# An encoder layer in one kernel: the first half rebuilt around contraction chunks and pairs of token tiles

## The reference, cut to what matters

```python
mod = (jax.nn.silu(c) @ w_ada + b_ada).reshape(bsz, 1, N_MOD, d)          # w_ada: 1024 x 6144
sh1, sc1, g1, sh2, sc2, g2 = (mod[:, :, i] for i in range(N_MOD))
h = x * (1 + sc1) + sh1
z = h @ w_in                                                              # 1024 x 1536: u | v | p
za = jax.nn.gelu(z[..., :2 * A_WIDTH])
u, v = za[..., :A_WIDTH], layer_norm(za[..., A_WIDTH:], v_norm_g, v_norm_b)
v = einsum('hqp,bnphc->bnqhc', w_spatial, v) + b_spatial.T[:, :, None]    # chunks of 128 tokens, 4 heads
a_out = u * v
pooled = multiscale_pool(z[..., 2 * A_WIDTH:])      # centred mean over 2, 4, 8, 16 tokens minus the token
b_out = einsum('bsgc,gcd->bsgd', pooled, w_pool) * pool_scale
mix = concatenate([a_out, b_out], axis=-1) @ w_out
x = layer_norm(ALPHA * x + g1 * mix, ln1_g, ln1_b)
h = x * (1 + sc2) + sh2
# then: routing to 2 of 32 experts for each token, the experts, and a last layer norm
```

## Time and profile before

| | |
|---|---|
| three runs | 1457.67, 1460.60, 1460.58 us (median 1460.58) |
| profiled execution, its own time | 1457.56 us |
| profiled execution, span from first to last instruction | 1455.8 us |
| TensorE busy, mean granted clock | 1266.5 us (87%), 0.940 |
| weight loads (PEld), VectorE, ScalarE, GpSimd busy | 1030.7, 932.9, 653.3, 280.3 us |
| HBM read, written | 297.47 MB, 39.37 MB |

### The profile page before, as it was taken

How to read it: one execution, slowest core, us unless ns; L and a number is a source line. 1 busy time by engine, 2 the same in 40 slices (tenths; PEclk the granted TensorE clock), 3 DMA queues, 4 the chain that set the end, 5 groups by cost and what they waited for, 6 DMA issues and landing times.

```text
span 1455.8 us, 22916 instructions
## 1 busy us (share of the span) xinstructions
PE 1266.5 (87%) x6239; PEld 1030.7 (71%) x6240; DVE 932.9 (64%) x1025; ACT 653.3 (45%) x635; POOL 280.3 (19%) x321
## 2 busy tenths in 40 slices
PE   4479999999789799426999999999999999999592
PEld 3367888788668588325888888888888888888440
DVE  7655544443356455595657875765478888888188
ACT  5532322111212112215556765665478888887222
POOL 6100000000024344241111211111112111222122
PEclk9889999999989899558999999999999999999896
DMA  9642231000233432634769996877689999998793
GB/s 296 246 143 93 96 102 57 18 29 1 92 125 116 144 115 101 243 132 168 263 245 344 402 366 226 307 261 269 226 342 396 398 397 395 388 406 310 307 348 138
DMA packets 111712, 329.44 MB, mean 226 GB/s; under 512 B 12192, under 2 KB 37952, under 8 KB 111680
## 3 DMA queue, kind: packets, MB, share of 16 engines
q1 hardware_dynamic: 98288, 288.63, 53.4%
q0 software_dynamic: 11520, 34.09, 6.3%
q10 hardware_dynamic: 1872, 6.29, 1.1%
HBM read 297.47 MB, written 39.37 MB: 231 GB/s over the span
## 4 chain that ended last, share of the span: by engine, by line
PE 77%; DVE 14%; DMA 3%; issue 2%; ACT 2%; POOL 1%; SPq 1%; DVEq 0%; POOLq 0%; ACTq 0%
PE bank L1320 21%; PE bank L1322 21%; PE bank L1321 21%; PE bank L1552 2%; PE bank L1342 1%; PE bank L1343 1%; PE bank L1516 1%; PE bank L1574 1%; DVE ada_l L944 1%; DVE hT L968 1%; DVE fin L1284 1%; DVE fin L1299 1%; DVE gated L1280 1%; PE bank L1407 1%; ACT ada_h L693 1%
## 5 line engine op out<-in xcount | busy, mean ns | idle before, releaser
L1220 DVE TENSOR_TENSOR gu_l<-gu_raw,gu_h x124 | 278.5, 2287 | 39.7 <-ACT gu_h L815 39.7
L1320 PE MATMUL bank<-gu_h,xT_h 128*128 (+1 forms) x624 | 248.1, 398 | 4.1 <-DVE xT_l L1239 4.1
L1322 PE MATMUL bank<-gu_h,xT_l 128*128 (+1 forms) x624 | 244.5, 392 | 0.0
L1321 PE MATMUL bank<-gu_l,xT_h 128*128 (+1 forms) x624 | 243.9, 391 | 0.0
L815 ACT ACTIVATE gu_h<-gu_raw (+1 forms) x128 | 238.4, 1924 | 5.2 <-issue 5.2
L1224 DVE TENSOR_TENSOR dn_l<-dn_raw,dn_h (+1 forms) x64 | 143.6, 2285 | 5.9 <-ACT dn_h L819 5.9
L1320 PEld LDWEIGHTS bank<-gu_h,xT_h 128*128 128x128 f32 x624 | 117.8, 189 | 28.1 <-DVE xT_l L1239 2.9
L1320 PE MATMUL bank<-win_h,hT_h 128*128 128x512 f32 x288 | 117.4, 408 | 22.5 <-DMA pool_s<-in_pool_scale 22.5
L1322 PEld LDWEIGHTS bank<-gu_h,xT_l 128*128 128x128 f32 x624 | 117.7, 189 | 25.5
L1321 PEld LDWEIGHTS bank<-gu_l,xT_h 128*128 128x128 f32 x624 | 118.0, 189 | 23.7
L819 ACT ACTIVATE dn_h<-dn_raw (+1 forms) x64 | 119.0, 1914 | 33.9 <-DVE table_i L1215 33.8
(11 more groups left out here) (226 smaller groups left out, 2144.5 us busy)
## 6 DMA issues: line engine op xcount, KB each, us to landing
gu_raw<-in_w_gate_up SPq DMA_DIRECT2D x128, 1024.0 KB, 7.5
dn_raw<-in_w_down SPq DMA_DIRECT2D x64, 1024.0 KB, 7.5
ada_raw<-in_w_ada SPq DMA_DIRECT2D x24, 1024.0 KB, 5.5
y<-y_rows SPq DMA_DIRECT2D x24, 512.0 KB, 5.4
win_raw<-in_w_in SPq DMA_DIRECT2D x8, 768.0 KB, 6.9
h_rows<-h SPq DMA_DIRECT2D x12, 512.0 KB, 2.7
x_rows<-x SPq DMA_DIRECT2D x12, 512.0 KB, 3.6
fin<-x_rows SPq DMA_DIRECT2D x12, 512.0 KB, 13.7
```

Source lines behind the costliest of these rows:

```text
L1220: nv.tensor_tensor(gu_slot(gu_l, e, c), gu_slot(gu_raw, e, c), gu_slot(gu_h, e, c).bitcast(F32), ALU.subtract).then_inc(S["gu_split_l"], 1)
L1320: mm(out, lh, rh, start=start, stop=False)
L1321: mm(out, lh, rl, start=False, stop=False)
L1322: return mm(out, ll, rh, start=False, stop=stop)
```

## The change

The first half, up to the mix stage, is rebuilt. Everything behind the mix of the last tile stays.

- **Opening by contraction chunk.** x tiles 0 and 1 are loaded and transposed first. For each chunk k of 8, SP loads two blocks of 128 columns of `w_ada` (shift and scale of these 128 channels, 0.5 MB each, rows of 512 bytes) and chunk k of W_in. `ada0_mm(k)` makes the chunk's shift and scale, VectorE and ScalarE modulate and split chunk k of x, and TensorE adds chunk k's products into all of u, v and p of the first pair. TensorE issues `ada0_mm(k + 1)` ahead of chunk k's products. VectorE makes `win_l` of chunk k - 1 in its turn k, behind the modulation of chunk k.
- **float32 conditioning.** `w_ada` is no longer split. Its blocks are the weights (128 x 128, float32) and the two columns of silu(c) are the moving operand: 16 float32 matmuls for 256 columns of `w_ada`, which give columns directly. `mod_columns`, `c_hl`, `pair_sum` and the high and low parts go. Eight blocks are in the opening and 16 late, at fixed points of pairs 1 to 3 (`ADA_POINTS`): seven bursts of two blocks and two of one.
- **Pairs.** The tokens go in 6 pairs of 256. u and p are made transposed, with W_in as weights and 256 moving columns (`chunk`), v as before (`v_part`). The spatial product comes out transposed too, its bias and `v_norm_b` go into an offset made once (`spatial_weights`), so that `a_transposes` and their copy go.
- **Pooling by running sums.** p lies transposed in `pbuf`, VectorE makes the window sums by four additions of shifted columns (`pool_p`), and the band matrices with their products (`pool_mm`) go. The last 8 tokens of a pair wait for the next one; at the end of a request they are made apart (`edge_mm`).
- **W_out in W_in's columns.** Its raw chunks go where u's and p's columns of W_in were, all at once, as soon as the last u and p are made, while v of the last pair is computed. The splits are ahead of the last `norm_v` and `gate_u` on VectorE. `mix(0)` is followed by the last pair's spatial and pool products, then `mix(1)`, then the last `edge_mm`; GpSimd's first `second` waits for that (`fb_made`).

```diff
+ADA_POINTS = {(1, "mid_u"): (0,), (1, "mid_v"): (1, 2), (1, "end_v"): (3, 4),
+              (2, "mid_u"): (5, 6), (2, "mid_v"): (7, 8), (2, "end_v"): (9, 10),
+              (3, "mid_u"): (11, 12), (3, "mid_v"): (13, 14), (3, "end_v"): (15,)}
...
@@ SyncE @@
+            sp.dma_start(xs[:], x_rows(0, 0)).then_inc(S["x_loaded"], 16)
+            sp.dma_start(xs_b[:], x_rows(0, 1)).then_inc(S["x_loaded"], 16)
...
             for k in range(KD):
+                if k >= ADA0_SLOTS:
+                    sp.wait_ge(S["ada_made"], k - ADA0_SLOTS + 1)
+                for m in range(2):
+                    c = m * D + k * P
+                    sp.dma_start(ada0[k % ADA0_SLOTS][:, m], w_ada[:, :, c:c + P]).then_inc(ada0_loaded[k % ADA0_SLOTS], 16)
                 if k >= WIN_SLOTS:
                     sp.wait_ge(S["win_l_made"], k - WIN_SLOTS + 1)
...
+            sp.wait_ge(S["u_made"], 2 * NP)
+            sp.wait_ge(S["p_made"], 2 * NP)
             for k in range(KD):
-                if k >= 4:
-                    sp.wait_ge(S["wout_l_made"], k - 3)
-                elif k == 0:
-                    sp.wait_ge(S["p_made"], NT)
-                sp.dma_start(wout_raw[k % 4][:], w_out[:, k, :]).then_inc(wout_loaded[k], 16)
+                sp.dma_start(wout_raw[:, k, 0::2, :], w_out[:, k, :].rearrange("p (a n) -> p a n", a=2)).then_inc(wout_loaded[k], 16)
@@ GpSimd @@
             plus_one(5)
+            pool.wait_ge(S["fb_made"], 2)
             second(0)
@@ VectorE @@
+            for k in range(KD):
+                dve.wait_ge(S["ada_made"], k + 1)
+                nv.tensor_tensor(mod[:, :, k:2 * KD:KD], ps[6 + k % 2][:, 4 * k:4 * k + 4].rearrange("p (c s) -> p s c", s=2),
+                                 cols[:, None, k:2 * KD:KD].to_broadcast([P, 2, 2]), ALU.add).then_inc(S["mod_made"], 1)
+                dve.wait_ge(S["mod_made"], k + 1)
+                high_gain(k)
+                nv.tensor_scalar(h_raw[0][:, k, :], h_raw[0][:, k, :], gain1[:, 0, k:k + 1], mod[:, 0, k:k + 1], ALU.mult, ALU.add).then_inc(S["k_mod"], 1)
+                if k >= 1:
+                    dve.wait_ge(S["win_h_made"], k)
+                    nv.tensor_tensor(win_l[:, k - 1, :], win_raw[(k - 1) % WIN_SLOTS][:], win_h[:, k - 1, :].bitcast(F32), ALU.subtract).then_inc(S["win_l_made"], 1)
+                dve.wait_ge(S["k_high"], k + 1)
+                nv.tensor_tensor(hT_l[0][:, k, :], h_raw[0][:, k, :], hT_h[0][:, k, :].bitcast(F32), ALU.subtract).then_inc(S["k_low"], 1)
...
+                n = PW - 1
+                for level in range(len(WINDOWS)):
+                    a, b = (pbuf, abuf)[level > 0], 1 << level
+                    st.done(nv.tensor_tensor(abuf[:, level:4, 0:n], a[:, level:4, 0:n], a[:, level:4, b:n + b], ALU.add))
...
+            norm_tile(0, 0, 0, prev=False)
+            edge_out(NP - 1, 6, 2)
@@ TensorE @@
+            def chunk(bank, j, part, k, s, start, stop):
+                out, c = ps[bank + j // 2][:, j % 2 * PT:(j % 2 + 1) * PT], slice(part * AW + j * P, part * AW + (j + 1) * P)
+                mm(out, win_h[:, k, c], hT_h[s][:, k, :], start=start, stop=False)
+                mm(out, win_h[:, k, c], hT_l[s][:, k, :], start=False, stop=False)
+                return mm(out, win_l[:, k, c], hT_h[s][:, k, :], start=False, stop=stop)
...
+            def ada0_mm(k):
...
+                for m in range(2):
+                    for kk in range(KD):
+                        last = mm(ps[6 + k % 2][:, 4 * k + 2 * m:4 * k + 2 * m + 2], ada0[k % ADA0_SLOTS][:, m, kk, :], c_cols[:, kk, :], start=kk == 0, stop=kk == KD - 1)
+                last.then_inc(S["ada_made"], 1)
...
+            ada0_mm(0)
+            for k in range(KD):
+                if k < KD - 1:
+                    ada0_mm(k + 1)
+                if k == KD - 1:
...
+                    transposes(2, 6, xs)
+                pe.wait_ge(S["k_low"], k + 1)
+                pe.wait_ge(S["win_l_made"], k + 1)
+                first, end = k == 0, k == KD - 1
+                for j in range(4):
+                    last = chunk(0, j, 0, k, 0, first and j % 2 == 0, end and j % 2 == 1)
...
+            transposes(3, 6, xs)
...
+            for i in range(1, NP):
+                s = i % 2
+                pe.wait_ge(S["hT_l_made"], 2 * i)
...
+            pe.wait_ge(S["u_gelu"], 2 * NP)
             mix(0, 0, first=True)
+            spatial(NP - 1)
+            pe.wait_ge(S["b_copied"], NP - 1)
+            w_pool_mm(NP - 1)
             mix(1, 1)
+            pe.wait_ge(S["b_copied"], NP)
+            edge_mm(6)
```

More of the change, by code:

```diff
@@ L130, in encoder @@
         r = Region(W0)
[L131 to L133 removed]
+        wout_raw = r.take("wout_raw", [P, KD, 3, AW])
+        wout_h = r.take("wout_h", [P, KD, 3, AW], F32R)
+        wout_l = Region(W0).take("wout_l", [P, KD, 3, AW], F32R)
         r = Region(W0)
@@ new lines, in ada_mm @@
+            def ada_mm(i, where):
+                for j, n in enumerate(ada_at(i, where)):
+                    pe.wait_ge(ada_loaded[n % 2], 16 * (n // 2 + 1))
+                    for c in range(ADA_N // P):
+                        at = 4 * j + 2 * c
+                        for kk in range(KD):
+                            last = mm(ps[ADA_BANK[where]][:, at:at + 2], ada_raw[n % 2][:, kk, c * P:(c + 1) * P], c_cols[:, kk, :], start=kk == 0, stop=kk == KD - 1)
+                    last.then_inc(S["ada_made"], 1)
@@ L1359, in _ @@
-            mod_columns(ps[4][:, 4 * N_ADA1 - 4:4 * N_ADA1], N_ADA1 - 1)
-            def transposes(t):
-                pe.wait_ge(S["x_loaded"], 16 * (t + 1))
-                if not (isinstance(t, int) and t == 0):
-                    pe.wait_ge(S["h_ready"], t)
-                for k in range(KD):
-                    last = nc.tensor.transpose(ps[k // 4][:, (k % 4) * P:(k % 4 + 1) * P], xs[:, k * P:(k + 1) * P], ident[:])
-                last.then_inc(S["xT_made"], 1)
-            def z_part(out, s, part, first=False):
-                c = slice(part * AW, (part + 1) * AW)
-                for k in range(KD):
-                    if first:
-                        pe.wait_ge(S["win_l_made"], k + 1)
-                    last = three(out, hT_h[s][:, k, :], hT_l[s][:, k, :], win_h[:, k, c], win_l[:, k, c], k == 0, k == KD - 1)
-                return last
@@ new lines, in _ @@
+            pe.wait_ge(S["x_loaded"], 32)
+            transposes(0, 0, xs)
+            transposes(1, 2, xs_b)
+            pe.wait_ge(S["rows_loaded"], 48)
+            nc.tensor.transpose(ps[7][:, 0:NCOL], col_rows[:], ident[0:NCOL, 0:NCOL]).then_inc(S["colsT_made"], 1)
+            pe.wait_ge(S["c_ready"], 1)
+            ada0_mm(0)
+            for k in range(KD):
+                if k < KD - 1:
+                    ada0_mm(k + 1)
+                if k == KD - 1:
+                    pe.wait_ge(S["x_loaded"], 48)
+                    pe.wait_ge(S["mod_made"], KD)
+                    transposes(2, 6, xs)
[4 more added lines that the diff above has]
+                    last = chunk(0, j, 0, k, 0, first and j % 2 == 0, end and j % 2 == 1)
+                    if end and j % 2:
+                        last.then_inc(S["u_made"], 1)
+                for half in range(2):
+                    last = v_part(half, k, 0, first, end)
+                    if end:
+                        last.then_inc(S["v_made"], 1)
+                for j in range(4):
+                    last = chunk(2, j, 2, k, 0, first and j % 2 == 0, end and j % 2 == 1)
+                    if end and j % 2:
+                        last.then_inc(S["p_made"], 1)
```

877 lines of the change are left out of this document (435 added, 442 removed).

## The result

| | before | after |
|---|---|---|
| median of the runs | 1459.9 us (four runs) | 1486.6 us (1485.4 to 1491.7) |
| ratio, 95% interval | | 1.0191, 1.0178 to 1.0205 |
| profiled execution, its own time; span | 1457.56; 1455.8 us | 1486.82; 1484.7 us |
| TensorE busy; mean granted clock | 1266.5; 0.940 | 1322.8; 0.900 |

The change makes the kernel 1.9% slower, 26.7 us by the medians. The forecast was +11 us by the profile; the profiled executions are 29.3 us apart.

A forecast was written before the change was run, and what follows sets the result against it. TensorE, 77% of the chain of waits, was taken as the bound. Pair 1 at 116.6 us, last v at 407.3 and mix tile 3 read at 469.1, 11 later than before, gave 1468.6 us; range 1411 to 1502.

The forecast's parts named there:

- VectorE's read of mix tile 3: Comparison point ahead of the untouched rest: forecast at 469.1 us against 458.15 before, 11 us later.
- With 3.75 us at the low clock the products take ... 5.9. A chunk's period is 12.0.: Opening: the clock falls before each chunk's products; 3.42 conditioning, 2.65 gap and 5.9 products make 12.0 us a chunk.
- Pairs 1 to 5: From pair 1's start at 116.6 us to the last v at 407.3, including 36.8 us lost to the clock.
- mix(0) starts 2 us after the last v: Way to the mix: `wout_l(0)` stands behind `norm_v(10)`, itself behind W_out copies on ScalarE; 14.3 us were lost before.
- The 5 us before mix(2): TensorE idles 5 us because GpSimd's `second(0)` waits for the edge product, holding tile 0's norm and `low_z(2)`.
- VectorE's gap: Opening: TensorE stands 2.65 us in each chunk, as VectorE starts `win_l` only after the next chunk's modulation.
- Rival "the clock holds": Conditioning bursts keep the clock high: chunks take 10.3 us, 54 us less in all, 1415 us; chance 0.18.
- Rival "the load does not run beside 256 columns": Weight loads of the 1152 256-column matmuls are not hidden: 123 us more, 1592 us; chance 0.05.

The follow-up runs named there:

- run 3: Changed kernel with `ada0_mm(k + 2)` instead of `ada0_mm(k + 1)` issued ahead of chunk k's products in the opening: 1462.2 us.
- run 4: Changed kernel with the opening's float32 matmuls of chunk k + 2 spread between the products of chunk k: 1496.0 us.
- run 5: Changed kernel with VectorE making `win_l` of chunk k - 1 ahead of its wait for `ada0_mm(k)`: 1453.1 us.
- run 6: Changed kernel with the opening's float32 matmuls spread between products and `win_l` made ahead of the wait for `ada0_mm`: 1456.3 us.
- run 7: Changed kernel with 128 moving columns instead of two in the opening's `ada0_mm`, order and idle kept: 1466.0 us.
- run 8: Changed kernel with GpSimd's `fb_made` wait moved from ahead of `second(0)` to ahead of its first h2: 1483.7 us.
- Run 9: Changed kernel with VectorE making W_out's first four low parts ahead of `norm_v(10)`: 1485.5 us.
- run 12: Changed kernel with all conditioning in bursts of 128 moving columns, `win_l` first, GpSimd's `fb_made` wait moved, W_out's first low parts ahead of `norm_v(10)`: 1393.5 us.
- run 2: Changed kernel with the late conditioning's moving operand widened from two to 128 columns, bursts and order kept: 1450.3 us.
- run 10: Changed kernel with late and opening conditioning spread between products, `win_l` first and GpSimd's `fb_made` wait moved: 1409.3 us.

## Why the prediction was right and wrong, point by point

The direction, the mechanisms and the places were right. The size was not: 11 us forecast at VectorE's read of mix tile 3, 26.8 measured. The terms that failed are sizes of the clock's cost.

- **"With 3.75 us at the low clock the products take ... 5.9. A chunk's period is 12.0."** This is the step that failed most: the term for the low clock in a chunk was too small. The 3.75 us have no row; the earlier trace rows show the clock rise 2.8 and 3.6 us behind a start. Here the low clock lasts 5.2 to 5.9 us into each chunk from the second on, and also reaches into the bursts (3.6 to 4.7 us between products and idle, where 3.42 was forecast). The period is (113.63 - 31.90)/6 = 13.6 us. Chunk 0 ended 1.3 us early, chunk 6 at 113.6 instead of 105.2; pair 1 started at 124.9 instead of 116.6: **8.3 us** of the miss.
- **Pairs 1 to 5**: 293.9 us where the terms give 290.7, **3.2** of the miss. That it is so little is in part luck: in the seven other traces in which TensorE has the same program here (runs 3 to 9) the pairs took 292.1 to 297.7 us. The seven double bursts took 69.6 us together against 47.9 at the high clock (21.7 more, forecast 19.9); the single bursts lost 1.9 and the dense work behind all of them some 19.0 (20.9, forecast 16.8). The clock cost 42.6 us here instead of 36.8, the other terms 251.3 instead of 253.9. Those held, 0.117 for 256 columns above all: in run 12 the pairs take 255.9, with their first 5 us still at the low clock, which is 2.3 more.
- **"mix(0) starts 2 us after the last v"**: 4.2, and its first matmuls ran at the low clock. The chain was the one named, longer: ScalarE made the fourth high part of W_out at 417.84, the GELU of v tile 10 behind it at 418.81, and then `norm_v(10)`, 419.41 to 421.7, stood ahead of the first low part. Run 9 takes `norm_v(10)` out of it and 0.23 is left. The 5 us before mix(2) were 5.95. mix(3) ended 65.9 us after the last v instead of 61.3: **4.6**.
- 8.3 + 3.2 + 4.6 = 16.1; the read of mix tile 3 missed by 15.9. The other 2.1 us are the untouched rest.
- **VectorE's gap** was forecast at 2.65 and measured at 2.67. As idle that is 18.6 us; run 5, which takes it out, won 33.5 by the medians and 30.6 by the profiled executions. An idle that touches a stretch with few moving columns cost its length and, here, another 11 us of low clock.
- **Rival "the clock holds"**: it did not hold, and runs 2 and 7 show what holding it is worth: 36.3 us late and 20.6 in the opening, 57 us together, against the 54 forecast. So the price of the whole was near, while the sum gave too little of it to the opening. Run 7 still has low clock in three chunks, so the opening's full price is above 20.6. The way to get the rival's time was open all along: move more columns.
- **Rival "the load does not run beside 256 columns"**: 0.118 us for each, so it does.

What stays open: why the low clock lasts 5.2 us in one chunk and 5.9 in the next, and why the mixed work of run 4 lifted the clock in chunk 4 and not in chunks 2 and 3; with that, a finer price than the 3 to 6 us by which executions differ. It was not tried.

## What to carry to other kernels

A stretch in which TensorE is busy with matmuls of two moving columns acted on the clock like a pause (1.00 at its start, 0.53 behind 3.3 us of it): look at the granted clock of the windows, not at the busy share, and where such matmuls can't go, repeat their moving columns; 128 cost 0.001 us more an instruction than two. Price an idle together with the thin work next to it: in the opening each alone brought the clock down in some chunks, both together in all. When a rebuilt part turns out slower, look for the order of two instructions on a second engine first: here one moved `win_l` was worth more than the whole loss.

## What the runs showed of the hardware that was not expected

- A float32 matmul instruction takes 0.110 us with 128 moving columns (64 in 7.06 us) and 0.109 with two (32 in 3.49, run 5): the columns are almost free up to there.
- Mixed work, two-column float32 matmuls between wide ones, held the high clock for 40 us (run 6). In the same order it stayed at the low one for 28 us in run 4 and then rose inside a mixed chunk, and in run 10 the clock fell inside mixed work at 106.3 us with no idle before it.
- The first 256-column matmul behind a two-column one costs more, the ones behind it 0.117, and the float32 pair accordingly less: a group of three and a pair took 43.70 - 43.13 = 0.57 us in run 4, 3 x 0.117 + 2 x 0.109, so going to and fro has no price of its own there, at the high clock.
- TensorE has the same program up to the last v in the changed kernel and in runs 8 and 9 and reached it at 418.80, 424.62 and 424.04 us: where the clock changes relative to the work differs between executions. The kernel of run 12, whose clock stays high up to the mix but for its start and 5 us at pair 1, ran within 2.4 us in four runs; the changed kernel's spread over 6.3.
